# Linear attention: exponents from products of the turned forget values, its rounds behind the scores

## What is computed

```python
def step(state, inp):
    qi, ki, vi, gi = inp
    cum = jnp.cumsum(gi, axis=2)
    diff = cum[:, :, :, None, :] - cum[:, :, None, :, :]
    decay = jnp.where(causal, jnp.exp(jnp.where(causal, diff, 0.0)), 0.0)
    scores = jnp.einsum('bhid,bhijd,bhjd->bhij', qi, decay, ki)
    last = cum[:, :, -1:, :]
    out = (jnp.einsum('bhij,bhjv->bhiv', scores, vi)
           + jnp.einsum('bhid,bhdv->bhiv', qi * jnp.exp(cum), state))
    state = (jnp.exp(last[:, :, 0, :, None]) * state
             + jnp.einsum('bhjd,bhjv->bhdv', ki * jnp.exp(last - cum), vi))
    return state, out
```

## Time and profile before

| | |
|---|---|
| median of 3 runs | 3171.48 us |
| lowest, highest | 3165.76, 3174.79 us |
| the profiled execution | 3173.36 us |
| its span (first to last instruction) | 3172.0 us |
| mean granted clock of TensorE | 0.949 |
| busy: PE, DVE, ACT, POOL | 2857.8, 1666.8, 1048.4, 728.8 us |

### The profile page before, as it was taken

The page is one execution under the profiler, slowest core; times in us unless marked ns, Lnnn a source line. Parts: engine busy times, 40 slices in busy tenths (PEclk is TensorE's granted clock), DMA queues, the critical chain, the costliest instruction groups (busy, mean ns, idle before and its releaser), DMA issues. The chain is left out here.

```text
span 3172.0 us, 39032 instructions
## 1 busy us (share of the span) xinstructions
PE 2857.8 (90%) x14792; PEld 2322.6 (73%) x14792; DVE 1666.8 (53%) x2848; ACT 1048.4 (33%) x2082; POOL 728.8 (23%) x458
## 2 busy tenths in 40 slices
PE   5999678989999999988798999889896989999988
PEld 4768578778888888867486787667683777877767
DVE  4170786534233134333888653676337796534865
ACT  3150654220000001201584540473005664421751
POOL 1233003223333333331022104103230212014021
PEclk9999778999999999999999999999899999999989
DMA  3111002111111211131121003114320220022032
GB/s 111 35 34 40 1 1 97 47 40 38 49 61 34 60 54 44 64 115 37 34 70 44 1 2 106 27 48 145 113 58 2 67 71 10 1 67 67 1 133 93
DMA packets 78972, 168.33 MB, mean 53 GB/s; under 512 B 15024, under 2 KB 33984, under 8 KB 78272
## 3 DMA queue, kind: packets, MB, share of 16 engines
q1 hardware_dynamic: 70336, 140.61, 13.5%
q10 hardware_dynamic: 8448, 25.18, 2.9%
HBM read 128.00 MB, written 20.97 MB: 47 GB/s over the span
## 5 line engine op out<-in xcount | busy, mean ns | idle before, releaser
L337 PE MATMUL psum<-H,ffn_W 128*128 128x512 f32 x672 | 262.8, 391 | 4.8 <-DVEq L1806 3.1
L339 PE MATMUL psum<-H,ffn_W 128*128 128x512 f32 x672 | 262.4, 390 | 0.0
L338 PE MATMUL psum<-H,ffn_W 128*128 128x512 f32 x672 | 262.4, 390 | 0.0
L2047 DVE TENSOR_SCALAR_CACHE_REDUCE MB<-OM,tk_mid 128x512 bf16<-128x512 f32 (+2 forms) x192 | 184.3, 1010 | 2.3
L523 POOL TENSOR_TENSOR tk_W<-tk_W 128x1024 fp32r<-128x1024 f32 (+1 forms) x38 | 76.6, 2017 | 422.3 <-ACT tk_W L475 422.3
L1573 POOL CAST ffn_W<-ffn_W 128x1024 fp32r<-128x1024 f32 (+1 forms) x77 | 65.2, 846 | 471.1 <-PE psum L339 469.0
L2016 ACT ACTIVATE MB<-OM,tk_mid 128x384 bf16<-128x384 f32 (+2 forms) x192 | 157.0, 819 | 49.1 <-DVE tk_mid L2044 44.4
L1787 DVE TENSOR_SCALAR ffn_Y<-ffn_G,ffn_par 128x1024 f32<-128x1024 f32 x21 | 21.4, 1021 | 288.2 <-ACT ffn_G L1760 288.2
L1760 ACT ACTIVATE ffn_G<-psum 128x1024 f32<-128x1024 f32 x21 | 21.6, 1031 | 446.0 <-PE psum L339 445.9
L1575 POOL TENSOR_TENSOR ffn_W<-ffn_W,ffn_W 128x1024 fp32r<-128x1024 f32 (+1 forms) x77 | 152.9, 1985 | 6.2
L337 PEld LDWEIGHTS psum<-H,ffn_W 128*128 128x128 f32 x672 | 126.8, 189 | 32.1 <-POOLq L1646 3.5
(11 more groups left out here) (453 smaller groups left out, 7580.8 us busy)
## 6 DMA issues: line engine op xcount, KB each, us to landing
OM<-in_w_feat SPq DMA_DIRECT2D x34, 512.0 KB, 4.6
tk_W<-in_w_feat SPq DMA_DIRECT2D x22, 512.0 KB, 3.6
ffn_W<-in_ffn_w_gate SPq DMA_DIRECT2D x21, 512.0 KB, 3.5
ffn_W<-in_ffn_w_val SPq DMA_DIRECT2D x21, 512.0 KB, 3.5
ffn_W<-in_ffn_w_down SPq DMA_DIRECT2D x42, 256.0 KB, 2.6
OM<-MB ACTq DMA_DIRECT2D x64, 128.0 KB, 2.7
OM<-OM ACTq DMA_DIRECT2D x64, 128.0 KB, 3.3
fin_W<-in_w_out SPq DMA_DIRECT2D x4, 2048.0 KB, 10.5
```

Source lines behind the costliest of these rows:

```text
L337: pe.matmul(out, a1, b1, start=start, stop=False)
L338: pe.matmul(out, a1, b2, start=False, stop=False)
L339: return pe.matmul(out, a2, b1, start=False, stop=stop)
L2047: own(dve.tensor_scalar(MB[:, self.keys(t)], IS[:, self.keys(t)], mid[:, n:n + 1], 0.0, ALU.is_lt, ALU.add, accum_out=self.cnt[:, n:n + 1]))
```

## The change

The exponents are no longer made by a scan and subtractions on DVE. PE turns the forget logarithms (`turn_forget`, tokens now on partitions), ACT and DVE split them into a rounded high part and a low rest (`high_of`, `rest_of`), and PE multiplies both by a constant table of zeros and ones (`sums`, 9 times 128 columns: seven levels, the whole sum, the sum of what follows), so that each exponent is a sum of logarithms between token and reference. A round (`round_of`) makes eight of the nine for one chunk, in banks 4 and 5, by four products of 128x512; ACT takes one exponential of 128x1024 (`bend`) for all eight. The ninth (`round_rest`, `bend_rest`) is made for four chunks at once. The table is loaded by SP at the stage's start and rounded by ACT. EL is copied from QE. AF's place is used for the two parts of the turned values.

The schedule is new too. Half u opens at step 4u - 5. In that step PE turns the keys of the half before, computes the next scores, and behind them makes rounds 0 and 1; in the next step rounds 2 and 3, behind the scores; in the third the rest, and DVE makes all 14 level products and QK, QE, KL in this one step; in the fourth, at its end, PE turns the forget values of the next half. The turned keys have bank 5 alone, and rounds wait until they are copied out. GpSimd no longer fills `keep`.

```diff
-                def prep(u, part):
+                def first_levels(u):
+                    dve.wait_ge(bent, ROUNDS * u + CH)
+                    for n in range(NL):
+                        weigh(u, n)
...
-                for part in range(3):
-                    prep(0, part)
+                rest_of(0)
+                first_levels(0)
+                rest_of(1)
+                last_levels(0)
...
-                        if prep_at(p, c):
-                            prep(*prep_at(p, c))
+                        if opened(step, 2) is not None:
+                            first_levels(opened(step, 2))
+                            last_levels(opened(step, 2))
+                        if opened(step, 3) is not None and opened(step, 3) + 1 < U:
+                            rest_of(opened(step, 3) + 1)
...
+                def bend(u, m):
+                    c = CH * (u % 2) + m
+                    act.wait_ge(sums, ROUNDS * u + m + 1)
+                    act.activation(XT[:, :, c * P:(c + 1) * P], kit.pair(2).rearrange("p (n t) -> p n t", n=NL + 1), ACT.Exp
+                                   ).then_inc(bent, 1)
...
+                act.wait_ge(sums_at, 16)
+                act.activation(M, M_in, ACT.Copy).then_inc(sums_high, 1)
+                high_of(0)
+                for m in range(CH):
+                    bend(0, m)
+                bend_rest(0)
+                high_of(1)
+                for n in range(4):
+                    part_heads(0, n)
+                bend(1, 0)
+                for n in range(4, NL):
+                    part_heads(0, n)
+                bend(1, 1)
                 keys_turned(0)
                 for p in range(NP):
                     for c in range(NT):
                         step = NT * p + c
+                        if opened(step, 0) is not None:
+                            u = opened(step, 0)
+                            keys_turned(u - 1)
+                            bend(u, 0)
+                            bend(u, 1)
+                        if opened(step, 1) is not None:
+                            bend(opened(step, 1), 2)
+                            bend(opened(step, 1), 3)
+                        if opened(step, 2) is not None:
+                            bend_rest(opened(step, 2))
...
                         act.wait_ge(out_done, step + 1)
                         act.activation(O[:, c, P * p:P * (p + 1)], kit.psum[:, 6, 0:P], ACT.Copy
                                        ).then_inc(out_taken, 1)
...
+                        if opened(step, 2) is not None:
+                            for n in range(NL):
+                                part_heads(opened(step, 2), n)
+                        if opened(step, 3) is not None and opened(step, 3) + 1 < U:
+                            high_of(opened(step, 3) + 1)
...
+                def round_of(u, m):
+                    pe.wait_ge(low, u + 1)
+                    if m:
+                        pe.wait_ge(bent, ROUNDS * u + m)
+                    keys_ahead = 0 if u == 0 or (u == 1 and m < 2) else u
+                    if keys_ahead:
+                        pe.wait_ge(kt_taken, keys_ahead)
+                    at = slice(m * P, (m + 1) * P)
+                    for c in range(2):
+                        to, cols = kit.psum[:, 4 + c, :], slice(c * HALF, (c + 1) * HALF)
+                        pe.matmul(to, LFT_high[:, at], M[:, cols], start=True, stop=False)
+                        last = pe.matmul(to, LFT_low[:, at], M[:, cols], start=False, stop=True)
+                    last.then_inc(sums, 1)
...
                         if step + 1 < NT * NP:
                             scores(*divmod(step + 1, NT))
+                        if opened(step, 0) is not None:
+                            round_of(opened(step, 0), 0)
+                            round_of(opened(step, 0), 1)
+                        if opened(step, 1) is not None:
+                            round_of(opened(step, 1), 2)
+                            round_of(opened(step, 1), 3)
+                        if opened(step, 2) is not None:
+                            round_rest(opened(step, 2))
                         pe.wait_ge(placed, step + 1)
...
                         last.then_inc(out_done, 1)
+                        if opened(step, 3) is not None and opened(step, 3) + 1 < U:
+                            turn_forget(opened(step, 3) + 1)
```

More of the change, by code:

```diff
@@ L95, in constants @@
     put("sin", np.concatenate([sin, -sin] * 2))
+    sums = np.zeros((P, 9, P))
+    row, col = j[:, None], j[None, :]
+    for n, b in enumerate(LEVELS):
+        ref = col // (2 * b) * 2 * b + b - 1
+        sums[:, n, :] = np.where(col > ref, (row > ref) & (row <= col), (row > col) & (row <= ref))
+    sums[:, 7, :] = row <= col
+    sums[:, 8, :] = row > col
+    put("sums", sums.reshape(P, -1))
     return c
@@ L915, in _, with gla_stage @@
                 own.wait()
-def gla_stage(kit, Q, K, LF, VA, VC, O, XT, X, spare, ident, level, heads, keep, closing):
+def gla_stage(kit, Q, K, LF, VA, VC, O, XT, X, LFT, ident, level, heads, sums_in, closing):
     nc = kit.nc
@@ new lines, in gla_stage @@
+    (sums_at, sums_high, turned, high, low, sums, bent, ends, lifted, spread, cleared, mixed, kt_done, kt_taken, scored,
+     placed, out_done, out_taken, upd_done, upd_taken, own_d, state_set) = (
+        kit.sem(f"gla_{n}") for n in (
+            "sums_at", "sums_high", "turned", "high", "low", "sums", "bent", "ends", "lifted", "spread", "cleared", "mixed",
+            "kt_done", "kt_taken", "scored", "placed", "out_done", "out_taken", "upd_done", "upd_taken", "own_d",
+            "state_set"))
@@ L952, in freed, with opens, opened @@
[L952 to L958, removed]
+    def opens(u):
+        return 4 * u - 5
+    def opened(step, behind):
+        u = (step - behind + 5) // 4
+        return u if 1 <= u < U and opens(u) == step - behind else None
     def spread_at(p, c):
         if p == 2 and CH <= c < CH + 3:
-            return 6, c - CH
+            return 6, ((0, 1), (2, 3), (4, 5, 6))[c - CH]
@@ L1131, in _ @@
             def _(act):
[L1132 to L1159, removed]
+                def high_of(u):
+                    act.wait_ge(turned, u + 1)
+                    act.activation(LFT_high, kit.psum[:, 4, :], ACT.Copy).then_inc(high, 1)
@@ L1229, in scores, with turn_forget @@
                     last.then_inc(scored, 1)
+                def turn_forget(u):
+                    if u:
+                        pe.wait_ge(bent, ROUNDS * u)
+                    for m in range(CH):
+                        c = CH * (u % 2) + m
+                        last = pe.transpose(kit.psum[:, 4, m * P:(m + 1) * P], LF[:, u // 2, c * P:(c + 1) * P], ident)
+                    last.then_inc(turned, 1)
+                def round_of(u, m):
[11 more added lines that the diff above has]
+                    last.then_inc(sums, 1)
@@ L1231, in keys, with round_rest @@
+                def round_rest(u):
+                    pe.wait_ge(bent, ROUNDS * u + CH)
+                    for m in range(CH):
+                        at = slice(m * P, (m + 1) * P)
+                        pe.matmul(kit.psum[:, 4, at], LFT_high[:, at], M[:, 8 * P:9 * P], start=True, stop=False)
+                        last = pe.matmul(kit.psum[:, 4, at], LFT_low[:, at], M[:, 8 * P:9 * P], start=False, stop=True)
+                    last.then_inc(sums, 1)
                 def keys(u):
                     pe.wait_ge(mixed, u + 1)
-                    if u >= 2:
-                        pe.wait_ge(kt_taken, u - 1)
+                    if u == 0:
+                        pe.wait_ge(bent, ROUNDS + 2)
@@ L1243, in _ @@
+                for m in range(CH):
+                    round_of(0, m)
+                round_rest(0)
+                turn_forget(1)
+                round_of(1, 0)
+                round_of(1, 1)
                 keys(0)
@@ L1899, in first_block @@
                   also=[(tables, d["constants"][:, FIRST_AT:ROPE_AT])])
-        keep = sbuf(nc, gla, "keep", [P, S])
+        LFT = [alias(f"LFT{n}", [P, HALF], FP32R, at_spare + n * HALF * 4) for n in range(2)]
+        M_in = alias("M_in", [P, 9 * P], FP32, shared)
         ff = FeedForward(kit, alias, d, at_raw, shared, at_high)
         closing = Closing(kit, BG, BG_high, BG_low, WB, WB_rounded, VA, VC, d["w_out"])
-        gla_stage(kit, Q, K, LF, VA, VC, OM, F1, F2, AF, ident, level, heads, keep, closing)
+        gla_stage(kit, Q, K, LF, VA, VC, OM, F1, F2, LFT, ident, level, heads,
+                  (M_in, d["constants"][:, SUMS_AT:SUMS_AT + 9 * P]), closing)
         gla.close()
```

142 lines of the change are left out of this document (48 added, 94 removed).

## The result

The changed kernel takes 3178.45 us (median of 17 runs, 3171.19 to 3182.8), the kernel before 3172.05 (17 runs, 3163.86 to 3176.26). The ratio is 1.0022, 95% interval 1.0015 to 1.0029: slower, by 0.2%, less than the 0.3% that the prediction called clear, and a third of the 19 us that it forecast. The profiled execution took 3177.65 us, its span is 3176.0.

A forecast was written before the change was run, and what follows sets the result against it. Quiet steps were taken as bound by PE, steps with preparation by DVE. Start +16, periods +6.8 and steps 19 and 20 -3.5 gave +19.3 on 3173.4, stated as 3192 us; 8-in-10 range 3170 to 3209.

The forecast's parts named there:

- The start: Attention stage up to step 2's output: table load, serial rounds and low clock add 16 us (bounds +9.5, +19).
- A period at full clock: Four loop steps, between output products, at 2.4 GHz: 25.2 us against 27.1 before.
- The fall of the clock: After each fourth step's stall: 3.6 us a period, making 28.8; four periods 115.2 against 108.4, +6.8.
- paid twice: Loop of the kernel before: each PE stall costs idleness and a slow step after it; 3.4 us, then 6.6 at 0.50.
- Steps 19 and 20: Loop steps without rounds, keys no longer waiting for DVE: 13.9 us before, change -3.5 (bounds -6.5 and 0).
- The tail: Last steps of the stage, same code: no change, but clock falls may shift them by +-2 us.
- the clock stays up: Rival, whole stage: PE holds 2.4 GHz throughout, sum -4.6 us, 3169 us; chance 0.15.
- DVE's time counts in full: Rival, loop: rounds hidden behind placing, five halves give 23 us back against 9.5 of the start, 3160 us; chance 0.09.
- The rounds hold the clock down: Rival, first and second steps: PE half busy, 34 us a period, +27, total 3213 us; chance 0.13.
- written off as not the bound: ACT in the loop: gets lighter by a few us, 14 part copies of 0.42 us remain, not the bound.

The follow-up runs named there:

- e7: Kernel before with three idle products in the second and sixth step's waits for DVE and before the keys: four periods 101.9 us, ratio 0.9963 to before.
- e3: Changed kernel with the first round of a step moved in front of the scores: four periods 105.5 us, ratio 1.0009 to the kernel before.
- e2: Changed kernel with idle products in PE's waits, in each fourth step and the start: four periods 100.2 us, ratio 0.9983 to the kernel before.
- e4: Changed kernel without the seven products by the keys from half 1 on: four periods 104.7 us, stage 213.1 us, one run, no ratio.

## Why the prediction was wrong

- **The start** (forecast +16): +15.2 on average of the traces. Right, by its steps: the table landed 3.8 us after its issue and ACT rounded it in 1.16, the rounds of half 0 follow one exponential apart, the first scores come at 31.5 us. The clock was down from the second round on:

```profile
335.80:343.90 8.10, 4.76 (x10) 2.33 (x8) 0.00 (x0) 2.94 (x3) 0.00 (x0) 0.50 0.01 2
```

- **A period at full clock** (25.2): 25.06. The steps 7.3, 6.7 and 11.2 were 7.31, 6.81 and 10.94; the stall 2.7 for 3.0.
- **The fall of the clock** (3.6 a period, four times: 14.4): this is the step that failed. It was sized as half of the 6.6 us of the earlier trace rows, plus something for the rounds. Measured are 1.64 us in three periods of four, 4.9. This term is 9.5 of the 10 us by which the periods missed (+6.8 forecast, -3.3 measured). The halving was right, since 1.64 is half of the 3.4 us that the clock was low; the length, copied from a step of the kernel before, and the fall in every period were not. The copied row was also misread as a cost: "paid twice" doesn't hold there, as e7 has that step at 1.00 in 6.15 us instead of 6.60.

  Why the low stretch is shorter stays open. In the kernel before the stall was 3.46 us, the clock fell within 0.2 us of its end and stayed low 6.8 us, in two periods of four 17.1; in step 6 it did so though PE was busy for 6.33 of 6.60 us. After, the stall was 2.7 us and the clock fell 0.2 to 1.7 us behind its end, by the three traces, and stayed low 3.4 us. In e3, with a stall of 2.8 us, it fell 0.7 to 0.9 us before the end and stayed low 10.2 us. Stall, place of the fall and what stands behind differ together, and no run varied one alone.
- **Steps 19 and 20** (-3.5): -4.9. Same term: low for less long.
- **The tail** (0, +-2): -1.1, +1.8, +2.9. Within its bounds but for the last.
- **The sum**: 15.2 - 3.3 - 4.9 + 1.2 = 8.2 us in the stage, and 6.4 in the medians.

Of the rivals, "the clock stays up" was nearest in time (3169) but is not what happened: the start had its full low stretch, the loop kept 1.00 in one period of four. A loop without a fall is e2's. "DVE's time counts in full" fell: DVE's busy time fell by 33 us over the span (1666.8 to 1633.9) and the periods by 3.3. "The rounds hold the clock down" holds for the start and not for the loop.

The other thing the prediction didn't see: ACT's 14 part copies end within 0.1 us of the output product that waits for DVE (e4). ACT was written off as not the bound, and at the fourth step it is a second one, as late as the first. This cost the forecast nothing.

## What to carry to other kernels

When work moves from an engine with a stall behind it to PE, read two things apart: the chain at full clock, which rows of the kernel before gave to within 0.2 us a period here, and the clock, whose low stretches at stalls of 2.7 to 3.5 us lasted from 3.4 to 17.1 us here and shouldn't be copied from another step. A pipeline that prepares its next part in the loop's gaps pays its full latency at the start, where there are no gaps; there an older, wider form of the same work can be the right one. And try idle products in PE's waits before judging a schedule, in both kernels: they turned this change from 0.2% slower to 0.2% faster, but gave the kernel before 0.4%.

## What the hardware showed that was not expected

- A stall of PE of 2.7 us is followed by a low clock in three periods of four and in one not, in the same code. The cost of a fall was 1.64 us with 3.4 us at the low level (after), and 4.0 with 10.2 us (e3).
- Two idle products in each stall of 2.7 us (1.96 us, with 0.90 left to wait), and others in the start, held the clock at 1.00 from DVE's first fill through all four periods (e2). In the kernel before three of them (2.82 us in the stall of 3.46), and three in front of the keys, brought 1.6 us a period (e7).
- A 128x128 product in the rounded format takes as long as one row of a plain one, and a plain one has two rows: eight rounded ones from 422.73 to the output at 423.66 are 0.116 us each, and the 14 rows of the seven score products from 373.62 to the next at 375.18 are 0.111 each (after).
- The time behind the stage varies by 13 us between traces (2629.3 to 2642.6), with no line changed there. A difference of 0.2% can't be read from one trace of each kernel.
